# GpSimd's part of each weight slab's low half: one instruction, or pieces of 512 columns

## What is computed

```python
for layer in range(2):
    want_ctx = layer < 1
    hx = modulate(rms_norm(x, norm1_g[layer]), sh1, sc1)          # hc likewise, of the context
    mx, mc = token_mixers(hx @ w_in[layer], hc @ w_in[layer], ...)  # attention A, attention B, pooling
    #   m = sigmoid(g_a)*(y_a @ w_pa) + sigmoid(g_b)*(y_b @ w_pb) + sigmoid(g_c)*(y_c @ w_pc);  m @ w_out
    x = x + g1 * mx
    hx = modulate(rms_norm(x, norm2_g[layer]), sh2, sc2)
    f = swiglu(h_all, w1, w3, w2) if layer == 0 else moe_swiglu(hx, router_w, router_b, w1, w3, w2)
    x = x + g2 * f
return rms_norm(x, final_g)
```

## Time and profile before

| what | value |
|---|---|
| median of 3 runs | 1977.72 us (1976.39 to 1979.67) |
| the profiled execution: time, and its span | 1974.67 us, 1972.9 us |
| PE busy | 1911.1 us, 97% of the span |
| PEld, DVE, ACT, POOL busy | 1390.7, 613.6, 450.3, 407.5 us |
| instructions on POOL, and those of L563 among them | 127, 88 |
| span's chain: PE, issue, POOL | 80%, 9%, 5% |

### The profile page before, as it was taken

How to read it: one execution, slowest core, us unless ns; L and a number is a source line. 1 busy time by engine, 2 the same in 40 slices (tenths; PEclk the granted TensorE clock), 3 DMA queues, 4 the chain that set the end, 5 groups by cost and what they waited for, 6 DMA issues and landing times.

```text
span 1972.9 us, 48520 instructions
## 1 busy us (share of the span) xinstructions
PE 1911.1 (97%) x22368; PEld 1390.7 (70%) x22369; DVE 613.6 (31%) x1199; ACT 450.3 (23%) x766; POOL 407.5 (21%) x127
## 2 busy tenths in 40 slices
PE   5999999999999999999999999999999999999997
PEld 3875788897888888977986666665666656666664
DVE  3356233163552544566542011020201102020112
ACT  4247432343222223456432000000000000000001
POOL 1500444425555544303540000000000000000000
PEclk9999999999999999999999999999999999999999
DMA  7352223234454564213578999999999999999990
GB/s 316 141 200 91 95 101 102 90 129 171 153 188 142 199 266 160 92 60 104 174 284 321 398 405 385 382 391 398 396 378 396 385 409 389 377 390 400 407 382 25
DMA packets 69999, 506.59 MB, mean 257 GB/s; under 512 B 7776, under 2 KB 7904, under 8 KB 9120
## 3 DMA queue, kind: packets, MB, share of 16 engines
q1 hardware_dynamic: 69408, 501.08, 65.6%
q0 software_dynamic: 384, 2.36, 0.3%
HBM read 502.36 MB, written 1.05 MB: 255 GB/s over the span
## 4 chain that ended last, share of the span: by engine, by line
PE 80%; issue 9%; POOL 5%; DMA 2%; ACT 1%; DVE 1%; SPq 0%; DVEq 0%; POOLq 0%; ACTq 0%
PE bank L1462 30%; PE bank L1474 14%; PE bank L913 10%; PE bank L915 10%; PE bank L914 10%; POOL w_lo L563 5%; DMA start_slab<-in_w_mod 1%; PE pv_bank L1247 1%; PE turned_pair L1229 1%; PE bank L948 1%; PE bank L1205 0%; PE bank L1476 0%; PE bank L1210 0%; ACT w_hi L1682 0%; PE turned_pair L1448 0%
## 5 line engine op out<-in xcount | busy, mean ns | idle before, releaser
L1462 PE MATMUL bank<-moe_slab,HE 128*32 128x256 f32 x10752 | 592.7, 379 | 1.3 <-DVE GT L2748 1.3
L1462 PEld LDWEIGHTS bank<-moe_slab,HE 128*32 128x32 f32 x10752 | 347.2, 110 | 232.7 <-DVE GT L2748 1.8
L563 POOL TENSOR_TENSOR w_lo<-slab,w_hi 128x2048 fp32r<-128x2048 f32 (+3 forms) x88 | 363.0, 4126 | 565.3 <-ACT w_hi L1682 565.2
L913 PE MATMUL bank<-H_HI,w_hi 128*128 128x512 f32 (+1 forms) x912 | 322.6, 354 | 10.1 <-POOL w_lo L563 4.7
L914 PE MATMUL bank<-H_LO,w_hi 128*128 128x512 f32 (+1 forms) x912 | 319.8, 351 | 0.0
L915 PE MATMUL bank<-H_HI,w_lo 128*128 128x512 f32 (+1 forms) x912 | 319.7, 351 | 0.0
L1474 PE MATMUL bank<-moe_slab,GE 128*32 128x256 f32 x4032 | 299.8, 379 | 0.0
L1476 PE MATMUL bank<-moe_slab,GE 128*32 128x256 f32 x1344 | 299.0, 379 | 0.0
L1474 PEld LDWEIGHTS bank<-moe_slab,GE 128*32 128x32 f32 x4032 | 165.6, 110 | 115.8
L2745 DVE TENSOR_TENSOR GT<-SE,bank 128x256 f32<-128x256 f32 x56 | 23.6, 421 | 633.0 <-ACT SE L2028 633.0
L1682 ACT ACTIVATE w_hi<-slab 128x2048 fp32r<-128x2048 f32 (+1 forms) x88 | 166.0, 1889 | 149.7 <-PE bank L915 149.2
(11 more groups left out here) (286 smaller groups left out, 2050.6 us busy)
## 6 DMA issues: line engine op xcount, KB each, us to landing
moe_slab<-in_moe_up SPq DMA_DIRECT2D x224, 1024.0 KB, 7.3
moe_slab<-in_moe_w SPq DMA_DIRECT2D x112, 1024.0 KB, 7.2
slab<-in_w_in SPq DMA_DIRECT2D x38, 1024.0 KB, 5.0
slab<-in_ffn_w SPq DMA_DIRECT2D x30, 1024.0 KB, 4.9
row_slab<-in_w_mod_rows SPq DMA_DIRECT2D x28, 1024.0 KB, 7.1
start_slab<-in_w_mod SPq DMA_DIRECT2D x8, 1024.0 KB, 17.7
slab<-in_w_proj SPq DMA_DIRECT2D x8, 1024.0 KB, 4.8
slab<-in_w_out SPq DMA_DIRECT2D x8, 1024.0 KB, 4.9
```

Of the source, the lines that this page charges most:

```text
L563: engine.tensor_tensor(lo, raw, hi.bitcast(F32), ALU.subtract).then_inc(done, 1)
L913: mm(out, lhs[0], rhs[0], start=start, stop=False)
L1462: ins = mm(outs[t // 2][32 * b:32 * b + 32, 256 * (t % 2):256 * (t % 2) + 256], rows[t], w[:, 256 * b:256 * b + 256], start=first and t != ...
```

## The change

POOL's part of a slab is made in instructions of at most 512 columns each, one behind the other, in place of one of up to 2048. Only the first waits, and only the last raises `lo_pool`. DVE's part stays one instruction, and the order on all engines stays as it was.

```diff
-        def low_part(eng, engine, key, lo_col, hi_col, done):
+        def low_part(eng, engine, key, lo_col, hi_col, done, piece=SLAB):
 
             n, at = SPLITS[key], SLABS[key]
             eng.wait_ge(hi_ready, n + 1)
             eng.wait_ge(slab_in[at % RING], 16 * (at // RING + 1))
-            raw, hi, lo = (t[:].rearrange("p k n -> p (k n)")[:, lo_col:hi_col]
-                           for t in (ring[at % RING], w_hi[SPLIT_PLACE[key]], w_lo[SPLIT_PLACE[key]]))
-            engine.tensor_tensor(lo, raw, hi.bitcast(F32), ALU.subtract).then_inc(done, 1)
+            for col in range(lo_col, hi_col, piece):
+                raw, hi, lo = (t[:].rearrange("p k n -> p (k n)")[:, col:min(col + piece, hi_col)]
+                               for t in (ring[at % RING], w_hi[SPLIT_PLACE[key]], w_lo[SPLIT_PLACE[key]]))
+                ins = engine.tensor_tensor(lo, raw, hi.bitcast(F32), ALU.subtract)
+            ins.then_inc(done, 1)
...
-                low_part(pool, nc.gpsimd, key, dve_cols(key), slab_size(key), lo_pool)
+                low_part(pool, nc.gpsimd, key, dve_cols(key), slab_size(key), lo_pool, SLAB // 4)
```

## The result

The changed kernel takes 1988.06 us in the median, the kernel before 1976.59 beside it; the ratio is 1.0042, with a 95% interval of 1.0032 to 1.0053: 8.3 us slower (6.3 to 10.5). The ratio goes by all executions; those of the changed kernel spread widely (1980.59 to 1990.94, eight of fifteen at 1988 and more), so that the two medians are 11.5 us apart. The predicted 1982.9 was 0.26% slower: the sign was right, the size too small. The predicted range ended at 1987: the median lies 1.1 us above it, while the ratio, on the 1977.72 that the prediction started from, makes 1986.0. The profiled execution took 1988.46 us, its span is 1986.5. L563 is L564 now, and lines behind it are two higher.

The account below looks back on a forecast made before the run. PE was taken to bound the kernel, busy 1911 of 1972.9 us. Terms 0.36 (layer 0's first gate slab), 1.46, 1.21, 0.36 and 1.8 sum to 5.2 us, added to the median 1977.7: 1982.9 us, range 1978.5 to 1987.

Parts of the forecast that it names:

- What PE waits for: Whole kernel: only PE's waits for low parts (7.2 us), `H_LO` (2.2 us) and places without slack can move the time.
- The price of a piece: Every POOL slab: each further piece costs 0.12 us from start to start; bounds 0 and 0.18.
- DVE's turns: At a piece's end a waiting DVE instruction goes first, delaying POOL by its length, such as 1.09 or 1.10 us.
- that rival: Whole kernel: pieces run as one, DVE gets no turn, only the pieces' cost of 2.3 us remains, 1980.0; chance 0.22.
- The second `w1` slab: Layer 0's feed-forward: pieces add 0.36 and one DVE `COND_ROW` product 1.10, together +1.46 us; bounds 0 and 2.6.
- Layer 1's first gate slab: At 906.33: DVE's half of the next slab enters between POOL's two pieces, +1.21 us; bounds 0 and 1.3.
- input slabs: Layer 1: one more piece in each of three slabs without slack, no DVE operation ready, +0.36 us; above, 0.8.
- gates: Layer 1's gates and projections: pieces +0.9, DVE's `M` sums in four slabs +0.9, together +1.8 us; bounds 0 and 3.
- `H_LO`: PE's two waits for DVE: first `H_LO` comes earlier, second is held by POOL's second piece; 0 us.
- output slabs: Two PE waits for POOL, 0.12 each, against DVE's earlier `M` sums; 0 us, bounds -1.1 and +0.3.
- loads: SyncE's slab refills start up to 1.5 us later, hidden because a slab is used 17 us on; 0 us.
- a rival for that place alone: Second `w1` slab: lower clock after a longer pause, 0.9 to 1.6 us, within more turns than counted, 1986.7; chance 0.11.

Follow-up runs that it names:

- experiment 4: Changed kernel with pieces only in slabs PE does not wait for, other slabs in one instruction; 1977.03 us, ratio 0.9996 to the kernel before.
- experiment 1: Pieces of 512 columns in layer 0's second `w1` slab alone, every other slab in one instruction; 1981.11 us, ratio 1.0012 to the kernel before.
- experiment 9: Kernel before, without pieces, but POOL makes its half of layer 1's first gate slab twice; 1983.51 us, ratio 1.0032 to the kernel before.
- Experiments 2: Changed kernel with pieces everywhere but in layer 0's second `w1` slab; 1983.95 us, ratio 1.0028 to the kernel before.
- experiment 6: Changed kernel with pieces only from layer 1's first gate slab on, none ahead of it; 1981.78 us, ratio 1.0028 to the kernel before.
- experiment 10: Kernel before, without pieces, DVE making 15/16 of layer 1's shared slabs and POOL 1/16 instead of half each; 1973.84 us, ratio 0.9985.
- experiment 8: Changed kernel with pieces of 256 columns instead of 512; 1989.72 us, ratio 1.0062 to the kernel before.

## Why the prediction came out as it did

- **What PE waits for.** Right. Outside the places that the prediction named the starts of PE's products drift apart only in stretches at 1.2 GHz, and pieces in hidden slabs cost nothing that can be told (experiment 4).
- **The price of a piece.** 0.12 predicted, 0.14 measured in three sizes.
- **DVE's turns.** The pieces do not run as one: both turns at 449 to 456 lie between pieces with no semaphore between them. The rule that led to that rival (the Trainium skill, GPSIMD Engine Reference, Instruction dispatch: a core of GpSimd goes on to the next instruction without a barrier) says nothing of what DVE does in between, and the trace shows that a DVE instruction which stands ready at a piece's end goes before the next piece.
- **The second `w1` slab.** This term failed: 1.46 predicted, 2.53 measured. The step was "I take it to be just too late", of the second product. It hung on the first: the prediction let it in after the second piece, and it got in after the first, by hundredths of a us, which freed DVE in time for another turn. The bound of 2.6 held. In experiment 1 the count was as predicted, with 1.41 us and a wait of 5.16 for a predicted 5.2.
- **Layer 1's first gate slab, input slabs, gates.** 1.13 for 1.21, 0.21 for 0.36, 1.44 for 1.8. In the gates the mechanism was right: the `M` sum that took 1.52 takes 0.42 (0.5 predicted), and its turn makes the second piece 0.26 us longer (0.28 predicted). Not foreseen was that the next `M` sum is then held, for 1.06 us instead of 0.42; PE shows no wait for it.
- **`H_LO`, output slabs, loads.** For `H_LO` zero predicted, -0.06 measured in both places. The mechanism was right: PE could start on the first 0.46 us earlier (429.30 instead of 429.76), and the second is held by the second piece. The output slabs grew by 0.18, within the bound of 0.3. A load lands in 5.0 us as before, and PE has no new wait for one.
- **The sum.** 5.2 predicted, 5.8 by the changed kernel's trace, 5.1 between the fastest executions. That it came so near is in part luck: the `w1` slab is 1.07 over its term, the others together 0.5 under theirs.
- **What was left out of the sum: the clock.** The prediction knew the lower clock behind the `w1` wait and put it into a rival for that place alone, at 0.9 to 1.6. It cost 0.4 there, and more at five later places, for which the prediction put nothing. From 1982.9 to the median of 1988.06 are 5.2 us: 0.6 more by the terms, 1.1 less since the median of before was 1976.59 this time, not 1977.72, and the rest, 5.7, is over the delays. By the ratio, which goes by all executions, 2.5 us are over the delays.
- **What is shown of the clock, and what isn't.** Shown in experiment 9: a wait that is 3.2 us longer ahead of the gates is followed by a stretch at 1.2 GHz that cost another 2.4. Experiments 2 and 6 measure more than the delays of their traces as well. Not shown: which of PE's waits are followed by such a stretch in an execution. The changed kernel had them behind waits that before has too, none of them longer than there, and experiment 6 has one where its program is still that of before. Nor do they go by the number of pieces, as far as one profile of each kernel tells: experiment 10, without any piece, shows two (granted clock 0.83 in 868 to 878 and in 902 to 912) and experiment 8, with twice as many, no more than two (near 791 and 877) behind 784 us. That they cost more on average with the pieces is how the ratios and the spread read; why stays open.

## What to carry to other kernels

Cutting an instruction so that another engine gets in between moves the wait, it does not remove it: ask which of the two engines the critical one waits for, and let that one finish in one go. Where two engines can do a piece of work only in turns, giving nearly all of a piece of work to the one that does it faster can beat an even split, because shares that cannot overlap add up. And where the matrix engine has no slack behind a wait, count more than the delay: measure what the same delay costs there when it is made by other means.

## What the runs showed of the hardware

- GpSimd and VectorE take turns on instructions that read two SBUF operands, instruction by instruction, with no semaphore needed: two turns of VectorE made a row of four pieces 6.98 us long instead of 4.94. Whoever stands ready at the other's end goes next, and 0.04 us decided in which gap a turn of 1.1 us fell (experiment 1).
- A subtraction of 128x2048 on GpSimd takes 4.56 us in one, 4.99 in four and 5.57 in eight instructions: 0.14 us each.
- Behind one and the same wait of PE, 2.90 us, the granted clock was 1.00 in one execution and 0.79 in another, with the same program up to there (experiment 6).
